# Two transformer blocks: the memory's norm moved into the first expert stage, its projections as direct fp32 products, two norms from one pass

## What is computed

```python
h  = rmsnorm_2(x, norm1_g_2)          # x = rmsnorm(x, final_g)
z  = h @ w_in_2                       # sk, sv, fq, fk, sq, mq, fv, gates
mn = rmsnorm_2(mem, mem_norm_g_2)     # mem: 256 memory rows, an input
mk, mv = split(mn @ w_mem_kv_2)       # 1024 x 512 each
```

## Time and profile before

| what | value |
|---|---|
| median of 3 runs | 2467.48 us (2466.64 to 2469.18) |
| the profiled execution: its time | 2467.22 us |
| its span in the trace | 2465.5 us |
| PE, DVE, ACT, POOL busy | 93%, 70%, 52%, 9% of the span |
| mean granted clock of PE | 0.983 |

### The profile page before, as it was taken

How to read it: one execution, slowest core, us unless ns; L and a number is a source line. 1 busy time by engine, 2 the same in 40 slices (tenths; PEclk the granted TensorE clock), 3 DMA queues, 4 the chain that set the end, 5 groups by cost and what they waited for, 6 DMA issues and landing times.

```text
span 2465.5 us, 47911 instructions
## 1 busy us (share of the span) xinstructions
PE 2296.1 (93%) x15320; PEld 2094.6 (85%) x15320; DVE 1723.3 (70%) x3637; ACT 1284.6 (52%) x2842; POOL 226.8 (9%) x285
## 2 busy tenths in 40 slices
PE   5998999999996699999899999999999976999998
PEld 4986899999995588888788888999999965888887
DVE  7675666888878966666645557458888779666665
ACT  3453345454556755555546653445454567555554
POOL 0000000000008900000000000000000059100000
PEclk8998999999999999999999999999999989999999
DMA  9750354555550065555334324445555510455554
GB/s 372 274 185 35 120 188 154 183 184 183 182 186 19 3 206 192 195 191 192 128 112 146 115 102 152 140 145 184 180 182 184 181 58 0 152 190 195 193 190 152
DMA packets 106078, 389.71 MB, mean 158 GB/s; under 512 B 12032, under 2 KB 12160, under 8 KB 105232
## 3 DMA queue, kind: packets, MB, share of 16 engines
q1 hardware_dynamic: 104688, 381.73, 45.0%
q10 hardware_dynamic: 992, 4.88, 0.5%
q0 software_dynamic: 320, 2.13, 0.2%
HBM read 387.64 MB, written 1.05 MB: 158 GB/s over the span
## 4 chain that ended last, share of the span: by engine, by line
PE 81%; POOL 9%; DVE 6%; ACT 2%; DMA 1%; issue 1%; SPq 0%; POOLq 0%; DVEq 0%; ACTq 0%
PE ps L581 19%; PE ps L548 16%; PE ps L543 16%; PE ps L545 16%; PE ps L585 9%; POOL scores L433 9%; DVE lo L1218 1%; DVE act_lo L1295 1%; DMA big<-ada_in 1%; DVE big L1302 1%; PE ps L695 1%; PE ps L662 1%; DVE act_hi L1294 1%; ACT big L1002 1%; PE ps L529 0%
## 5 line engine op out<-in xcount | busy, mean ns | idle before, releaser
L926 ACT ACTIVATE hi<-raw 128x512 fp32r<-128x512 f32 x1356 | 776.8, 620 | 81.0 <-PE ps L548 78.5
L1218 DVE TENSOR_TENSOR lo<-raw,hi 128x512 fp32r<-128x512 f32 x844 | 546.9, 689 | 170.9 <-ACT hi L926 170.1
L543 PE MATMUL ps<-act_hi,hi 128*128 128x256 f32 x3376 | 552.5, 286 | 13.3 <-DVE act_lo L1295 6.1
L548 PE MATMUL ps<-act_hi,lo 128*128 128x256 f32 x3376 | 546.2, 284 | 11.4 <-DVE lo L1218 11.4
L545 PE MATMUL ps<-act_lo,hi 128*128 128x256 f32 x3376 | 544.7, 284 | 0.0
L543 PEld LDWEIGHTS ps<-act_hi,hi 128*128 128x128 f32 x3376 | 468.6, 193 | 26.9 <-issue 13.8
L548 PEld LDWEIGHTS ps<-act_hi,lo 128*128 128x128 f32 x3376 | 468.5, 193 | 12.8 <-DVE lo L1218 12.8
L545 PEld LDWEIGHTS ps<-act_lo,hi 128*128 128x128 f32 x3376 | 468.0, 193 | 0.0
L1494 DVE TENSOR_TENSOR lo<-raw,hi 128x512 fp32r<-128x512 f32 x512 | 329.8, 688 | 131.5 <-ACT hi L926 124.2
L961 ACT ACTIVATE big<-ps 128x256 f32 (+1 forms) x346 | 133.2, 385 | 527.5 <-PE ps L548 527.4
L581 PE MATMUL ps<-hi,act_hi 128*128 128x512 f32 x1024 | 398.8, 389 | 0.0
(11 more groups left out here) (183 smaller groups left out, 1400.5 us busy)
## 6 DMA issues: line engine op xcount, KB each, us to landing
raw<-u SPq DMA_DIRECT2D x256, 512.0 KB, 4.1
raw<-v SPq DMA_DIRECT2D x256, 512.0 KB, 3.4
raw<-front SPq DMA_DIRECT2D x166, 512.0 KB, 3.5
big<-ada_in SPq DMA_DIRECT2D x48, 512.0 KB, 5.2
big<-biasA_in ACTq DMA_DIRECT2D x1, 2048.0 KB, 9.9
xT<-xT_in ACTq DMA_DIRECT2D x1, 1024.0 KB, 10.2
big<-keys_in ACTq DMA_DIRECT2D x1, 1024.0 KB, 13.3
scores<-memT_in POOLq DMA_DIRECT2D x1, 1024.0 KB, 5.3
```

Of the source, the lines that this page charges most:

```text
L543: pe.matmul(out_ap, hi_l(k), hi_r(k), start=(first and k == 0), stop=False, skip_group_check=True)
L548: mm = pe.matmul(out_ap, lo_l(k), hi_r(k), start=False, stop=(last and k == n - 1), skip_group_check=True)
L926: act.activation(hi[:, s, :, :], raw[:, rs, 4 * h:4 * h + 4, :], ACT.Copy).then_inc(hi_done, 1)
L1218: dve.tensor_tensor(lo[:, s, :, :], raw[:, rs, 4 * h:4 * h + 4, :], hi[:, s, :, :].bitcast(F32), ALU.subtract).then_inc(lo_done, 1)
```

## The change

- mk and mv become kind "F": their units are not split. PE multiplies the fp32 weights in `raw` by the fp32 `memT` directly, 8 fp32 matmuls a unit (`mem_run`). Slots of `raw` come free by a new counter, `mem_used`, and the units no longer count in `hi_done`, `lo_done` and `used`.
- The memory is normalised in place during V of the first block: ACT squares one tile in each of the units 4 to 11, DVE adds the eight tiles in three steps in units 13 to 15, PE sums over partitions with one product by `ones` after unit 15, ACT forms the root in unit 16, DVE scales one tile in each of the units 18 to 25. The first seven groups of V are written out instead of one, in both blocks. The table set for logarithm and exponential is loaded before V.
- The final norm and `norm1_2` come from one pass: ACT squares each tile of x twice, once with the final gain as its scale; DVE adds each set in three steps; PE sums both after the third unit of mk. With r the reciprocal root of the first mean square, the second mean square is r squared times the second sum. DVE scales x by the product of both gains and both roots and splits it, then applies the final norm to the residual.
- All fillers between V and `sk` are gone. ACT takes the outputs of mk and mv in a list of its own, with the roots between the third and fourth unit of mk.

```diff
-    Run("mk", "T", 4), Run("mv", "T", 4), Run("sk", "T", 1), Run("sv", "T", 1),
+    Run("mk", "F", 4), Run("mv", "F", 4), Run("sk", "T", 1), Run("sv", "T", 1),
...
-CHAINED = ("va", "qkb", "vb", "gates1", "mv", "sv", "fq_fk_sq_mq", "fv", "gates2")
+CHAINED = ("va", "qkb", "vb", "gates1", "sv", "fq_fk_sq_mq", "fv", "gates2")
...
+        half += 0 if r.kind == "F" else 2 * r.units
...
-NORMS = ["norm1", "norm2", "mem", "final", "norm1_2", "norm2_2"]
+NORMS = ["norm1", "norm2", "norm2_2"]
+MEM_SQUARE_AT, MEM_TREE_AT, MEM_SUM_AT, MEM_RSTD_AT, MEM_APPLY_AT = 4, 13, 15, 16, 18
+V_PEEL = 7
...
+                first, count = RUNS["mk"].unit0, RUNS["mk"].units + RUNS["mv"].units
+                if is_static(n) and first <= n - RAW < first + count:
+                    sp.wait_ge(mem_used, n - RAW - first + 1)
+                elif block == 2 and not (is_static(n) and n - RAW < first):
+                    sp.wait_ge(lo_done, (n - RAW + 1 - count) * 2)
+                else:
+                    sp.wait_ge(lo_done, (n - RAW + 1) * 2)
...
+            def mem_run(name, after=None):
+
+                r = RUNS[name]
+                pe.wait_ge(mem_ready, KT)
+                for u in range(r.units):
+                    n, o = r.unit0 + u, r.out0 + u
+                    pe.wait_ge(raw_in[n % RAW], 16 * (n // RAW + 1))
+                    pe.wait_ge(taken, o - 1)
+                    for k in range(KT):
+                        mm = pe.matmul(po[o % 2], raw[:, n % RAW, k, :], memT[:, k, :], start=(k == 0), stop=(k == KT - 1))
+                    mm.then_inc(mem_used, 1)
+                    if after is not None:
+                        after(u)
...
+                def after_value(u):
+
+                    if b == 1 and u == MEM_SUM_AT:
+                        pe.wait_ge(mem_tree, 3)
+                        pe.matmul(bw[1][:, 0:T], ones[:, :], mem_sq[:, 0, :], start=True, stop=True).then_inc(mem_sum, 1)
+
+                run(f"v{b}", after=after_value, peel=V_PEEL)
...
-            norm_sum("mem")
-            norm_sum("final")
-            keep_busy(9)
-            run("mk", "mem")
-            run("mv")
+            def after_key(u):
+
+                if u == 2:
+                    for i in range(2):
+                        pe.wait_ge(fin_tree, 3 * i + 3)
+                        pe.matmul(bw[i][:, 0:T], ones[:, :], fin_sq[i][:, 0, :], start=True, stop=True).then_inc(fin_sum, 1)
+
+            mem_run("mk", after_key)
+            mem_run("mv")
             to_tokens("mv")
-            keep_busy(6)
-            norm_sum("norm1_2")
-            keep_busy(17)
             pe.wait_ge(act_ready, 2 * EV["norm1_2"] + 2)
...
+                if b == 1:
+                    act.preload_act_table_set(LN_EXP)
                 act.wait_ge(w_done, 64 * b)
+
+                def after_value(u):
+
+                    kt = u - MEM_SQUARE_AT
+                    if kt == 0:
+                        act.wait_ge(mem_in_s, 16)
+                    if 0 <= kt < KT:
+                        act.activation(mem_sq[:, kt, :], memT[:, kt, :], ACT.Square).then_inc(mem_sq_s, 1)
+                    if u == MEM_RSTD_AT:
+                        act.wait_ge(mem_sum, 1)
+                        link(act.activation(mem_r[:, 0, :], bw[1][:, 0:T], ACT.Ln, bias=eps[:, :], scale=1.0 / D))
+                        act.activation(mem_r[:, 1, :], mem_r[:, 0, :], ACT.Exp, scale=-0.5).then_inc(mem_rstd, 1)
 
                 def body(g):
                     for j in range(GROUP):
...
                                        ACT.Copy).then_inc(ahi, 1)
                         for h in range(2):
                             weight_hi(r, g, j, h)
-
-                groups(act, r, body)
+                        if b == 1 and is_static(g):
+                            after_value(u)
+
+                groups(act, r, body, peel=V_PEEL)
...
-            act.wait_ge(mem_in_s, 16)
-            norm_squares("mem", memT)
-            norm_squares("final", xT, (x_tile, 0))
-            norm_rstd("mem")
-            norm_rstd("final")
-            last_out = run("mk", to(mkT), defer=True)
-            run("mv", to(values["mv"][0]), lead=last_out)
+            def mem_out(name, dst, u):
+
+                act.wait_ge(mem_used, RUNS[name].unit0 - RUNS["mk"].unit0 + u + 1)
+                act.activation(dst[:, u, :], po[(RUNS[name].out0 + u) % 2], ACT.Copy).then_inc(taken, 1)
+
+            for kt in range(KT):
+                act.wait_ge(x_tile, kt + 1)
+                act.activation(fin_sq[0][:, kt, :], xT[:, kt, :], ACT.Square).then_inc(fin_sq_s, 1)
+                act.activation(fin_sq[1][:, kt, :], xT[:, kt, :], ACT.Square, scale=col("final_g", kt)).then_inc(fin_sq_s, 1)
+            for u in range(3):
+                mem_out("mk", mkT, u)
+            act.wait_ge(fin_sum, 1)
+            link(act.activation(fin_r[:, 0, :], bw[0][:, 0:T], ACT.Ln, bias=eps[:, :], scale=1.0 / D))
+            act.activation(fin_r[:, 1, :], fin_r[:, 0, :], ACT.Exp, scale=-1.0).then_inc(fin_r1, 1)
+            act.activation(fin_r[:, 2, :], fin_r[:, 0, :], ACT.Exp, scale=-0.5).then_inc(fin_r1, 1)
+            act.wait_ge(fin_q, 1)
+            link(act.activation(fin_r[:, 3, :], fin_r[:, 3, :], ACT.Ln, bias=eps[:, :], scale=1.0 / D))
+            act.activation(fin_r[:, 4, :], fin_r[:, 3, :], ACT.Exp, scale=-0.5).then_inc(fin_r2, 1)
+            mem_out("mk", mkT, 3)
+            for u in range(4):
+                mem_out("mv", values["mv"][0], u)
             copy_tokens("mv")
-            act.wait_ge(x_ready, 3)
-            act.wait_ge(act_ready, 2 * EV["mem"] + 2)
-            norm_squares("norm1_2", xT)
-            norm_rstd("norm1_2")
...
+                def after_value(u):
+
+                    if u == MEM_TREE_AT:
+                        dve.wait_ge(mem_sq_s, KT)
+                    if 0 <= u - MEM_TREE_AT < 3:
+                        square_tree(mem_sq, u - MEM_TREE_AT, mem_tree, u - MEM_TREE_AT + 1)
+                    kt = u - MEM_APPLY_AT
+                    if kt == 0:
+                        dve.wait_ge(mem_rstd, 1)
+                    if 0 <= kt < KT:
+                        dve.scalar_tensor_tensor(out=memT[:, kt, :], in0=memT[:, kt, :], scalar=col("mem_g", kt),
+                                                 in1=mem_r[:, 1, :], op0=ALU.mult, op1=ALU.mult).then_inc(mem_ready, 1)
...
+            def square_tree(squares, level, ready, count):
+
+                n = KT >> (level + 1)
+                dve.tensor_tensor(squares[:, 0:n, :], squares[:, 0:n, :], squares[:, n:2 * n, :], ALU.add)\
+                    .then_inc(ready, 1)
+                dve.wait_ge(ready, count)
...
+            dve.tensor_tensor(final_gain[:, :], g_final, cols[:, COLS["norm1_g_2"][0]:COLS["norm1_g_2"][0] + 8], ALU.mult)
...
-            norm_apply("mem", memT, lambda kt: col("mem_g", kt))
-
-            dve.wait_ge(n_rstd, NORMS.index("final") + 1)
+            for i in range(2):
+                dve.wait_ge(fin_sq_s, 2 * KT - 1 + i)
+                for level in range(3):
+                    square_tree(fin_sq[i], level, fin_tree, 3 * i + level + 1)
+            dve.wait_ge(fin_sum, 2)
+            dve.wait_ge(fin_r1, 1)
+            dve.tensor_tensor(fin_r[:, 3, :], bw[1][:, 0:T], fin_r[:, 1, :], ALU.mult).then_inc(fin_q, 1)
+            dve.wait_ge(fin_r1, 2)
+            dve.wait_ge(fin_r2, 1)
+            link(dve.tensor_tensor(fin_r[:, 5, :], fin_r[:, 2, :], fin_r[:, 4, :], ALU.mult))
+            for c in (0, 4):
+                for kt in range(c, c + 4):
+                    ins = dve.scalar_tensor_tensor(out=tmp[:, kt, :], in0=xT[:, kt, :], scalar=final_gain[:, kt:kt + 1],
+                                                   in1=fin_r[:, 5, :], op0=ALU.mult, op1=ALU.mult)
+                    ins.then_inc(n_scaled, 1)
+                dve.wait_ge(n_scaled, 16 + c + 4)
+                split_part(c, tmp[:, c:c + 4, :])
             for kt in range(KT):
                 ins = dve.scalar_tensor_tensor(out=xT[:, kt, :], in0=xT[:, kt, :], scalar=col("final_g", kt),
-                                               in1=norm_at["final"][1][:, 1, :], op0=ALU.mult, op1=ALU.mult)
+                                               in1=fin_r[:, 2, :], op0=ALU.mult, op1=ALU.mult)
             link(ins)
             dve.engine_nop().then_inc(x_ready, 1)
-            run("mk")
-            run("mv")
-            dve.wait_ge(taken, RUNS["sk"].out0)
 
             dve.wait_ge(swa_d, 1)
             for h in range(8):
                 ins = dve.tensor_scalar(biasS[:, h, :, :], dist, -8.0 * 2.0 ** -(h + 1), None, ALU.mult)
             link(ins)
             dve.engine_nop().then_inc(swa_d, 1)
-            norm_apply("norm1_2", xT, lambda kt: col("norm1_g_2", kt))
```

(37 more changed lines are left out.)

10 lines of the change are left out of this document (5 added, 5 removed).

## The result

The changed kernel takes 2436.97 us (median of 4, 2436.38 to 2440.11) against 2468.05 us for the kernel before in the same job (4 runs). The ratio is 0.9877, interval [0.986, 0.9894]. The span of a traced execution runs from its first to its last instruction.

What follows compares the result with a forecast made beforehand. PE was taken to bound the kernel (81% of the chain), so gains lie where it waits or does fillers. Seam -27.6 plus V 0.44 gave -27.2 from 2467.22; with 0.26 for the median, 2440.2 us, range 2438.0 to 2446.5.

Steps and rivals of the forecast that it cites:

- Each stop of PE that was to go: Between V and sk: PE's waits before mk, the 4.54 us stop, and the 14.94 us for norm1_2 disappear.
- the chain of the one pass: Behind mk and mv: trees end 0.8 us before PE's sums, split 9 us before PE wants it; not hidden, 2%.
- V pays: In V of the first block: one extra PE sum, 2 records, costs 0.44 us on the path.
- ACT's activations of unit 17: In V: ACT waits for the memory's sum, comes about 1.35 us late; costed at nothing, 1.35 at most.
- SP's queue: Weight loads of mv and sk: they go out as slots come free and land before they are wanted.
- the written-out groups: V in both blocks: groups written out instead of looped cost nothing.
- The seam: From start of the transposes after V to sk's first product: 63.93 us before, 27.6 us less forecast.
- I take 0.2225: mk and mv: us per fp32 record back to back, bounds 0.216 and 0.2267; eight units 28.48 us.
- norm sums: PE's fp32 sums in the seam before, each with a wait and weight load: 0.223 us a record, guide for mk and mv.
- the key scores' extra 0.008: fp32 products of 128 columns with new weights: 0.116 us against 0.108, so weight loads add some 0.008.
- -27.6 + 0.44: Whole kernel: the seam's gain plus V's extra sum, -27.2 us against the profiled 2467.22.
- 0.85 for the record: Low end of the range: allowance of 0.85 us should a record of mk and mv take 0.216.

Runs made afterwards that it cites:

- fp32 products alone: Kernel before with only mk and mv made fp32 products of raw weights, memory still normalised behind V, all fillers kept: 2464.3 us, ratio 0.9987.
- two passes: Changed kernel with the second squares taken of the residual after the final norm, a separate pass still behind the products: 2438.0 us.
- units twice: Changed kernel with each product of mk and mv made twice into the same output: 2469.0 us (1 run).
- 1.3 us of fillers: Changed kernel with 3 fillers of PE added behind the transposes of mv: 2440.9 us.

## Why the prediction was wrong

**Direction and mechanism** held. Each stop of PE that was to go went; the chain of the one pass fits (trees 0.7 before they are wanted, forecast 0.8; split 8.9, forecast 9); V pays 0.48 (forecast 0.44); ACT's activations of unit 17 are 1.3 late and cost nothing; SP's queue costs nothing that a trace shows, nor do the written-out groups (349.3 for the second V in both kernels).

**The seam** was undersized: 28.4 against 27.6. The step is "I take 0.2225" a record, "nearest to the norm sums". It is 0.216, the lower bound; with 132 records that is 0.9. The norm sums at 0.223 have a wait ahead of each product, which mk and mv have not, and the key scores' extra 0.008 (on products half as long) does not carry over to 256 columns.

**What made it wrong** is a term that the sum did not have. "-27.6 + 0.44" took all that stands behind sk as unchanged, at nothing and without a reason. Behind sk the traces of the changed kernel take 2.0 to 2.6 less than those of before, with one fall of the clock in the second block's front instead of three. The forecast used the clock for the seam alone, though the mean of 0.983 before stands for some 84 us at 1.2 GHz, of which the seam holds 6.8 (1228.9 to 1235.7). A range should have held one to two us either way for it; downwards mine left 0.85 for the record, 0.44 for V and 0.8 for scatter, and the result is 1.0 below. With 0.8 for the seam and 2.0 to 2.6 for the part behind sk the forecast of 2440.2 would have been 2436.8 to 2437.4, though the part ahead of V, 0.7 to 3.4 longer in the traces of the changed kernel, is in neither sum.

**Why there are fewer falls** is shown in part only. Each fall stands in its trace, and the code behind sk does not set their number. The two waits in swa_o lie at the same place behind sk in all 13 traces, while the beat on which the clock falls slides against the code from one execution to the next. That the changed kernel had one fall in both its traces and the old one three in both may thus be luck in part. It is not luck alone: the mean granted clock averages 0.985 over the eight executions of the changed kernel and 0.982 over the 13 of before, and the 6.8 us of the seam make 0.001 of that. What ties the one to the other stays open.

**Slips in the working.** 2467.22 - 27.2 + 0.26 is 2440.3, not 2440.2, and the low end worked out from its three terms is 2438.1, not 2438.0. Nothing hangs on either.

**What is left.** Seam, V and the part behind sk give 28.4 - 0.5 + 2.0 to 2.6 = 29.9 to 30.5 of the 31.1. The profiled executions of the changed kernel, 2440.11 and 2437.99, are each the slowest of their four, and the ones of before, 2467.22 and 2467.38, lie below its median of 2468.0. The granted clock goes with it: 2440.11 had 0.983, the three beside it, 2436.4 to 2437.4, had 0.985 or 0.986.

**Where the 28.4 came from**, in the order of the runs: fp32 products alone 2.8 (63.93 to 61.12); with them, taking the residual's norms behind the products 13.0 (to 48.12); the memory's norm into V 12.6 (to 35.51). The middle step includes fillers taken away and the roots' new order. The run with two passes shows that the one pass is not needed when the memory's norm is in V; without that it was not tried. Whether mk and mv, still split into fp32r halves (23.0 us of products instead of 27.6, at 0.48 for four records), would be faster behind a norm made in V was not tried: the halves of the memory need room beside V's own, and DVE, by an estimate from 0.62 a half (2.50 for four at 1249.36), another 10 us in the seam.

## What to carry to other kernels

Where two chains of small operations stand between stages that keep PE full, look for a stage ahead with idle time on ACT and DVE, and for products that depend on neither chain: here each was worth some 13 us of PE's waits for 0.5 us in V. A product straight on fp32 costs 20% more PE time than three fp32r products at 256 columns (3.45 against 2.88 us a unit), and pays where the split would stand on the path. Where PE has waits of one or two microseconds, each can bring a fall of the clock or not, by 1 to 1.5 us of time each, from one edit to the next and from one execution to the next. Before a difference of a few us is explained by the edit, cut both traces at the same places, count the falls, and trace each kernel more than once.

## What the runs showed of the hardware

- Two waits of 0.5 and 1.5 us, with 1.2 us of products between them, end 216.3 and 219.0 us behind sk in all 13 traces. Behind them the clock fell in five (before twice, units twice, 1.3 us of fillers, fp32 units only) and not in eight, and neither the code nor the place counted from the kernel's start tells which. That agrees with what the Trainium skill says in TensorE: Matmul & The Clock Gate (section What's actually happening), that the chip judges activity on a beat of its own, not on the kernel's.
- From one fall to two the time behind sk grows by 1.4 to 1.5 us, at equal time at the lower clock later on; from two to three by 1.1, and by 1.8 in the run with the units twice.
- The mean granted clock of each execution is worth reading before its time: within one kernel 0.002 of it went with 2 us of 2468.
- Fresh fp32 weights of 128 columns for each product of 256 columns add nothing to 0.216 us a record. Loads of 0.19 us run under products of the same rows. The rule weighed in the prediction, of the Trainium skill's TensorE: Matmul & The Clock Gate (section What overlaps and what doesn't), that a load overlaps only for another row group, does not hold here.
- 512 columns of fp32r take 0.2267 us a matmul, while an fp32 record over 256 columns takes 0.216, so 0.011 more for the same number of column passes, if a record is two of them. This was not looked into.
